# Eight-core mLSTM and stick-breaking decoder: TensorE without waits on its own semaphore, and output-weight pieces loaded at another place

## The reference, cut to what matters

```python
kv = x @ kv_w                        # 2048 x 4096: one shared K and V, 16 heads of 128
q, z = split(x @ b_w_in)             # 2048 x 4096: own queries and a gate
for each head, for each query t:     # strictly causal
    beta[t,s] = sigmoid(q[t] . k[s] / sqrt(128))          s < t
    a[t,s]    = beta[t,s] * prod(1 - beta[t,j], s < j < t)
    att[t]    = sum_s a[t,s] * v[s]
y = (att * silu(z)) @ b_w_out        # 2048 x 2048
x = LayerNorm(alpha * x + y)         # alpha = 4 ** 0.25
```

## Time and profile before

| | us |
|---|---|
| runs shown: median (lowest to highest), 3 | 2776.19 (2773.04 to 3223.05) |
| profiled execution, its own time | 2772.03 |
| span of its slowest core, first to last instruction | 2770.7 |
| spans of the eight cores | 2762.1 to 2770.7 |
| busy on that core: TensorE (PE) / weight loads (PEld) | 2604.8 / 1281.4 |
| busy: VectorE (DVE) / ScalarE (ACT) / GpSimd (POOL) | 1926.2 / 1073.1 / 166.7 |

### The profile page before, as it was taken

How to read it: one execution, slowest core, us unless ns; L and a number is a source line. 1 busy time by engine, 2 the same in 40 slices (tenths; PEclk the granted TensorE clock), 3 DMA queues, 4 the chain that set the end, 5 groups by cost and what they waited for, 6 DMA issues and landing times.

```text
span 2770.7 us, 48074 instructions; the slowest of 8 cores (2762.1 to 2770.7 us)
## 1 busy us (share of the span) xinstructions
PE 2604.8 (94%) x13562; PEld 1281.4 (46%) x13827; DVE 1926.2 (70%) x3318; ACT 1073.1 (39%) x2299; POOL 166.7 (6%) x311
## 2 busy tenths in 40 slices
PE   6999999999999998999999999999999999956997
PEld 2555555555555653444444444444444444423443
DVE  3555555555555446772888889888988988857777
ACT  2444444444444542332333333433343334323111
POOL 1000000000000110000000000000000000000000
PEclk9999999999999999999999999999999999978999
DMA  9703214231213237885566666667667665471453
GB/s 150 129 10 71 39 41 86 55 55 25 55 30 66 43 91 212 213 225 100 94 105 113 104 112 112 107 109 113 104 106 114 114 101 103 82 198 33 162 182 130
DMA packets 416784, 283.55 MB, mean 102 GB/s; under 512 B 356240, under 2 KB 380688, under 8 KB 412432
## 3 DMA queue, kind: packets, MB, share of 16 engines
q1 hardware_dynamic: 395792, 180.26, 29.8%
q0 software_dynamic: 20736, 100.21, 21.2%
HBM read 239.00 MB, written 50.07 MB: 104 GB/s over the span
## 4 chain that ended last, share of the span: by engine, by line
PE 79%; DVE 7%; issue 6%; DMA 4%; ACT 3%; SPq 1%; DVEq 0%; POOL 0%; ACTq 0%; another core or an unknown queue 0%; POOLq 0%
PE PS L882 33%; PE PS L326 12%; PE PS L593 11%; PE PS L476 7%; PE PS L610 5%; PE PS L960 4%; PE PS L1032 4%; DVE M L495 2%; DMA M<-xT 1%; ACT M L487 1%; DVE M L492 1%; DMA M<-mid_a 1%; PE PT L693 1%; ACT M L685 1%; SPq L133 1%
## 5 line engine op out<-in xcount | busy, mean ns | idle before, releaser
L882 PE MATMUL PS<-M 128*128 128x512 bf16 x3994 | 963.3, 379 | 37.7 <-PE PS L960 2.2
L982 DVE TENSOR_TENSOR_SCAN M<-M 128x513 f32<-128x513 f32 (+3 forms) x640 | 699.4, 1099 | 164.7 <-ACT M L963 154.8
L882 PEld LDWEIGHTS PS<-M 128*128 128x128 bf16 x4096 | 380.2, 97 | 542.8 <-issue 156.0
L963 ACT ACTIVATE M<-PS 128x512 f32<-128x512 f32 (+3 forms) x640 | 339.8, 535 | 493.4 <-PE PS L960 343.7
L326 PE MATMUL PS<-M 128*128 128x512 bf16 x2005 | 459.2, 386 | 40.3 <-DVE M L353 18.1
L593 PE MATMUL PS<-M 128*128 128x512 bf16 x1969 | 472.4, 379 | 4.8 <-ACT M L613 0.6
L990 DVE TENSOR_TENSOR M<-M 128x512 bf16<-128x512 f32 (+3 forms) x640 | 365.9, 593 | 0.0
L326 PEld LDWEIGHTS PS<-M 128*128 128x128 bf16 x2048 | 200.5, 99 | 288.6 <-issue 63.2
L593 PEld LDWEIGHTS PS<-M 128*128 128x128 bf16 x2048 | 188.6, 98 | 204.8 <-issue 3.3
L476 PE MATMUL PS<-M 128*128 128x512 bf16 x989 | 244.0, 389 | 22.7 <-DMA M<-xT 19.6
L603 DVE SCALAR_TENSOR_TENSOR M<-M 128x256 f32<-128x256 f32 x128 | 54.4, 425 | 277.1 <-ACT M L601 277.1
(11 more groups left out here) (120 smaller groups left out, 1853.6 us busy)
## 6 DMA issues: line engine op xcount, KB each, us to landing
M<-b_wp POOLq DMA_DIRECT2D x64, 512.0 KB, 6.3
y<-M SPq DMA_DIRECT2D x59, 512.0 KB, 3.5
M<-a_g POOLq DMA_DIRECT2D x8, 2048.0 KB, 18.3
M<-x SPq DMA_DIRECT2D x32, 512.0 KB, 5.3
M<-y SPq DMA_DIRECT2D x22, 512.0 KB, 4.6
M<-M SPq DMA_TRANSPOSE x680, 2.5
M<-a_qk POOLq DMA_DIRECT2D x16, 512.0 KB, 8.3
M<-a_v POOLq DMA_DIRECT2D x8, 1024.0 KB, 22.5
```

The costliest lines, as they stand in the source:

```text
L882: kb.op("pe", lambda: P_.matmul(PS[bank][:, :], lhsT=WR[w][:, c, :], rhs=XTv[:, tb, c, :], start=(c == 0), stop=(c == KC - 1)), R=[("WR", ...
L963: kb.op("act", lambda: A_.activation(out=U[us][:, 512 - w:512], in_=PS[zb][:, 0:w], func=AF.Sigmoid, scale=-scale), R=[("ps", zb)], W=[("U ...
L982: kb.op("dve", lambda: V.tensor_tensor_scan(out=rev(P[ps], 512 - w, 513), data0=rev(U[us], 512 - w, 513), data1=d1, initial=init, op0=ALU. ...
```

## The change

`_wait` returns without a wait when TensorE would wait for its own semaphore. And in heads 2 to 11 the piece of the output weights is asked for at unit 6 instead of unit 4, and only after VectorE's subtraction of the last lane of the unit before (the last writer of buffer `("Ab", (4k-1) % 10)`).

```diff
@@ -41,6 +41,8 @@
         if dep is None:
             return
         sn, v = dep
+        if sn == "pe" and e == "pe":
+            return
         if self.seen[e].get(sn, 0) >= v:
             return
         self.seen[e][sn] = v
@@ -850,9 +852,9 @@
-        def ld_wob(i):
+        def ld_wob(i, after=()):
             nb, q = i // 4, i % 4
-            kb.dma("pool", f"wob{i}", WOB[i], b_wo[nb][:, q * 4:(q + 1) * 4, :], W=[("WOB", i)])
+            kb.dma("pool", f"wob{i}", WOB[i], b_wo[nb][:, q * 4:(q + 1) * 4, :], W=[("WOB", i)], A=list(after))
@@ -1093,8 +1095,8 @@
-                if pos == 4 and 2 <= h < 12:
-                    ld_wob(h - 2)
+                if pos == 6 and 2 <= h < 12:
+                    ld_wob(h - 2, [("Ab", (4 * k - 1) % NA)])
```

## The result

The changed kernel takes 2746.19 us, median of four runs; beside it the kernel before ran from 2773.04 us up. The ratio is 0.9887, 95% interval 0.9838 to 0.9936: 1.1% faster. Medians of single runs take in disturbed executions that the comparison leaves out, so kernels are compared here by their ratios and by their traces. The profiled execution took 2748.3 us, span 2747.0 us (core 3; the other cores 2716.6 to 2741.1).

What follows compares the result with a forecast made beforehand. TensorE, busy 94% of the span, was taken as the bound, VectorE next. 2772.0 - 75 (self-waits) - 2 (other waits) + 5 (late transposes) = 2700, forecast 2704 us as median; own range 2690 to 2715, with rivals to 2742.

Steps and rivals of the forecast that it cites:

- What one wait costs, and how many: TensorE's self-waits before projections in the fifteen heads: 212 lose 0.31 us each, 60 lose 0.15, together 75 us to win.
- Sum, "+5" given back: 2772.0 - 75 - 2 + 5 = 2700 us; the 5 is lost again to late transposes at heads' last units, bounds 0 and 10.
- the 2 us for other lines: Gain from removed self-waits outside the fifteen heads' projection, in the mLSTM stage and at L326; bounds 0 and 14.
- What is late next: In the fifteen heads, TensorE comes sooner for transposes needed by output matmuls; 5 us given back in all.
- Two places are tight: Transposes before the third weight tile, margin 0.6 us, and in a head's last unit, margin 1.1; elsewhere no loss counted.
- place (b): Last unit of a head: VectorE's lag and TensorE's pace take 1.4 to 1.8 us from margin 1.1, costing 0.3 to 0.7.
- The loads that are moved: Ten 512 KB pieces asked for between a head's second and third weight tile, with a new wait on VectorE; price 0.
- VectorE takes over the pace: Rival: TensorE goes in step with VectorE through each head's last two units, 42 us given back, 2741 us; chance 0.08.
- The moved pieces collide: Rival: pieces run into the third weight tile, transposes land later, 31 us over ten heads, 2735 us; chance 0.11.
- The change doesn't do what it says: Rival: the gap before projections stays without the wait, as the array can't take the next weights; 2776 us; chance 0.04.
- Slower: the clock: Rival: nearly gapless TensorE in the fifteen heads drops to 1.2 of 2.4 GHz; 2979 us if four heads; chance 0.04.
- The rule that I weighed: DMA queues take turns by packet, so a 2.5 us transpose takes about 5 beside a load; the trace's 8.4 was kept.

Runs made afterwards that it cites:

- e10: Against e9: the sums of the output matmuls alternate between two PSUM banks; 0.975 of the kernel before, median 2704.06 us.
- e1: Against the kernel before: only TensorE's waits on its own semaphore removed, the ten pieces left right behind a weight tile; ratio 0.9954.
- e9: Against the change: output matmuls three units behind the scores instead of two, a fourth transpose buffer, last head's buffer order mended; 0.9777 of the kernel before.
- e3: Against the change: 60 of the 64 loads of projection weight tiles left out, so weights are wrong; 0.9791 of the kernel before.
- e6: Against the change: the ten pieces loaded in a row before the first head's attention; 0.9959 of the kernel before, stage 1063.2 to 1073.3 us.
- e11: Against the kernel before: self-waits and old place of the pieces kept, output matmuls three units behind, fourth transpose buffer; ratio 0.9994.

## Why the prediction was wrong

**What one wait costs, and how many: right.** The steps of 0.22 and 0.16 us are there, the 75 us (212 times 0.31 and 60 times 0.15, as counted) vanished from the places named, and e10 shows them at the end of the clock: 74.4 us.

**Sum, "+5" given back: wrong, by 46.** The working was made for one execution: 2700 us. The profiled one took 2748.3, 48 more. Of that, the stage: 1098.1 against the 1121.9 - 75 + 5 = 1051.9 that the sum implies, +46 (33 in the mean of the eight cores). The 46 are accounted for: the 1047.5 us of e10, 43 of stops and 7 of slow matmuls make 1098. The stage began 9.8 us earlier than in the execution of before and what comes after it took 9.8 more (349.1 against 339.3), in which the stop behind the last of the fifteen heads grew from 18.8 to 26.5 us; the 2 us for other lines are the rest.

**The step that failed** is "What is late next", with its sentence "Two places are tight". I looked at one head on one core, took the margins found there (0.6 and 1.1 us) and subtracted from them what TensorE gains on VectorE. The two places themselves, units 6 and 9, cost 3.6 us on core 3, inside my 5. (Two slips there change little: unit 6's last transpose, issued at 1816.4, lands at 1822.6, so that margin was 0.3; and a fifteenth of 14.3 us is 0.95, not 0.8.) The costly places were others: unit 1, unit 5 and unit 8, whose last transposes had landed 1.3 to 6.3 (median 6.2), 3.2 to 5.6 and 3.2 to 4.2 us ahead of use in the kernel before (heads 0 to 13, six cores). Those margins looked safe because I treated landing time as fixed at 2.5 or 8.4 us for each place. It jumps: TensorE's matmuls free a tile's buffer and so set when the tile is asked for, VectorE sets when a transpose is issued. Before, a head's second tile was asked for 19.0 us after the head's start (median), and unit 1's last transpose was issued 0.5 to 1.4 us ahead of it; now the tile is asked for at 17.8 us, and the transpose is issued anywhere from 0.7 us ahead of it to 1.9 behind (heads 1 to 13 of all cores). Unit 5's transposes lie beside the moved piece. In head 2 on core 3, unit 1's 6.3 us of margin became 0.3 and a stop of 2.5: of these 8.5 us, 6.0 are the longer landing, which the prediction had at nothing, and 2.5 VectorE's lag, of which it had 1.4 to 1.8 at its place (b).

**The loads that are moved: the price 0 was wrong, the direction right.** "Each has two units, about 14 us, until it is wanted" counts from the scores; VectorE's lag and the landing use up most of it, and 3.2 to 5.6 us of it were spare. The piece itself lands nearly as I took it, after 7.2 us in the median on core 3 and 5.4 to 8.4 on all cores, for my 6.1. But it stops unit 5's output matmuls in nine of the ten heads on core 3, 10.7 us, and in two to eight heads, 2.6 to 7.6 us, on the other cores with complete records. The cover named on POOL held: in head 5, behind the piece, POOL waits another 6.03 us for TensorE before it may ask for the next tile. At the old place, though, the pieces cost more: e1's stage is 21 us longer than the change's in the mean of the cores.

**The rivals.** *VectorE takes over the pace* did not come in its form: no score matmul in the stage waits for ScalarE by more than 1.5 us in all, and e10 goes at 69.96 us a head with VectorE at 95%. But VectorE did hold TensorE at a place that no rival had: the single bank, 12.2 us (12.8 of waits in e9, 0.6 in e10). In the kernel before it lay hidden beside the self-waits. That this rival's time, 2741 us, came nearest to the measured one is luck. *The moved pieces collide* came nearest in kind, but its mechanism is another one: pieces and tiles collide with transposes, not with each other, and the tiles do more of it (the mean stage is 25 us shorter without the tiles, e3, and 17 without the pieces, e6). *The change doesn't do what it says* is out. *Slower: the clock*: the mLSTM stage stayed at 1.00 with 894.36 of 905 us busy, and e10's stage at 1.00; the fall came only after stops, as below.

The rule that I weighed may have been read wrongly. I made "twice as long" of the turns by packet (the Trainium skill, "DMA: Bandwidth & Descriptors", Queues, rings and completion order). It counts packets, not bytes, and the two queues here, in 1458 to 1460 us of the changed kernel (packets, MB, share of the engines' time), have packets of very different size:
```profile
q1 hardware_dynamic: 461, 0.10, 24.9%
q0 software_dynamic: 9, 0.04, 21.8%
```
Some 220 bytes for the transposes, about 4 KB for the load. If these are the packets of the rule, the load moves twenty times the bytes turn by turn, and a transpose that starts behind it ends with it: the 8.4 us agree with the rule so read, and so do e6's 39.3. That this is the cause of the late landing is argued; no run here changed the packets. That late landings beside loads cost the time is shown, by e3 and e9. Why the cores differ among themselves (1074.9 to 1098.1 us with the same program) was not taken apart: in e9 and e10, where no output matmul waits for a transpose, all eight agree to 0.2 us.

## What to carry to other kernels

When a bound engine is made faster, ask of every transfer between it and its neighbours not only how much margin it has, but what sets its order among the other loads, and whether a changed order makes its landing jump. A margin is safe only if it is larger than the jump and the growing lag together: here 6 and 2.5 us, and unit 1's 6.3 were not enough. Then give the consumer one more buffer and one more stage of delay before, or together with, the faster pace: alone the third unit gave nothing (e11) and the faster pace 1%, together 2.2% (e9), and with the second bank 2.5%.

## What was not expected of the hardware

After a stop of about 3 us TensorE's granted clock fell to the lower of its two levels, 1.2 of 2.4 GHz, for a while: 0.66 in the mean of 1962 to 1967 us of the changed kernel, in the window shown above, behind the stop at 1962.22, with 1.00 in the stretches on both sides (1955 to 1962, 1967 to 1975):
```profile
1959.15 0.33 PE L962 MATMUL PS<-M 128*128 128x384 bf16 x1
1962.22 1.01 PE L1034 MATMUL PS<-M 128*128 128x512 bf16 x2 [2.75 <-DMA M<-M]
1963.03 1.91 PE L884 MATMUL PS<-M 128*128 128x512 bf16 x4
```
Four projection matmuls take 1.91 us where four take 1.03 in the timeline further up. On this core it happened five times in the stage, behind its five longest stops (2.6 to 3.8 us); behind two others, of 2.5 and 2.6 us, the matmuls kept full speed. So a stop costs more than its length: this unit took 11.1 us where 6.59 is its length without stops, 2.9 of the 4.5 in the stop, 1.6 in slower matmuls. Stops under a microsecond, as at 1774.50 in e9, are followed by matmuls of full speed.
